# The output-gate projection taken out of the recurrence and made in ten half-width pieces between the units of the attention

## What is computed

```python
q_m, k_m, v_m, o_m, gates, q_d, k_d, v_d = project(h, w_in)       # one projection, 8 column groups
h_m = mlstm_bidirectional(q_m, k_m, v_m, gates, C0, n0, m0)       # recurrence in chunks of 128 tokens, both ways
h_d = blocked_diff_attention(q_r, k_all, v_all, lam)              # softmax map 0 minus lam * softmax map 1

def mix_output(h_m, o_m, h_d, lam_init, g_m, g_d, w_out):
    hm = head_rmsnorm(h_m).reshape(B, S, MLSTM_WIDTH) * g_m * jax.nn.sigmoid(o_m)
    hd = head_rmsnorm(h_d).reshape(B, S, DIFF_WIDTH) * g_d * (1.0 - lam_init)
    return jnp.concatenate([hm, hd], axis=-1) @ w_out
```

## Time and profile before

| what | us |
|---|---|
| median of three runs | 767.49 (765.44 to 768.3) |
| the profiled execution, its own time | 762.14 |
| its span | 760.3 |
| PE busy over the span | 671.4 (88%) |
| DVE busy over the span | 377.6 (50%) |
| recurrence, first group's scores to last group's values | 169.08 to 339.39 |
| attention, from there to the first product of the output projection | 339.39 to 419.21 |

### The profile page before, as it was taken

The page is one execution under the profiler, slowest core; times in us unless marked ns, Lnnn a source line. Parts: engine busy times, 40 slices in busy tenths (PEclk is TensorE's granted clock), DMA queues, the critical chain, the costliest instruction groups (busy, mean ns, idle before and its releaser), DMA issues.

```text
span 760.3 us, 7675 instructions
## 1 busy us (share of the span) xinstructions
PE 671.4 (88%) x2660; PEld 363.1 (48%) x2660; DVE 377.6 (50%) x784; ACT 169.1 (22%) x413; POOL 143.0 (19%) x153
## 2 busy tenths in 40 slices
PE   3899999999999999995789989992999999999920
PEld 3343573355555555443567544552544444444420
DVE  3226533413545522668987256668244423444238
ACT  6001100011212111114677221122022111221123
POOL 1042000022021100002632100003133113332061
PEclk9999999999999999998999999996899999999965
DMA  8999708422140302104000395001599999999357
GB/s 295 386 285 328 283 2 302 170 74 79 28 139 15 126 26 81 44 0 167 0 2 0 150 369 201 28 28 43 172 359 333 355 350 375 364 342 352 128 192 277
DMA packets 63058, 137.88 MB, mean 181 GB/s; under 512 B 4678, under 2 KB 11198, under 8 KB 63028
## 3 DMA queue, kind: packets, MB, share of 16 engines
q1 hardware_dynamic: 52344, 109.80, 40.9%
q0 software_dynamic: 5280, 15.63, 5.9%
q10 hardware_dynamic: 5404, 12.06, 4.0%
HBM read 122.70 MB, written 14.74 MB: 181 GB/s over the span
## 4 chain that ended last, share of the span: by engine, by line
PE 73%; DVE 11%; DMA 6%; issue 4%; ACT 2%; POOL 1%; SPq 1%; ACTq 0%; POOLq 0%; DVEq 0%
PE PS L1504 26%; PE PS L1821 15%; PE PS L1836 7%; PE PS L1496 5%; PE PS L1699 3%; DMA PR<-in_w_ada 3%; PE PS L1535 2%; PE PS L1688 1%; DVE PR L1003 1%; DMA PR<-scratch_mod 1%; PE PS L1618 1%; DVE stat L1136 1%; PE PS L1814 1%; PE PS L1592 1%; PE PS L1743 1%
## 5 line engine op out<-in xcount | busy, mean ns | idle before, releaser
L1504 PE MATMUL PS<-RING,hT 128*128 128x512 f32 x480 | 216.4, 598 | 0.8 <-DVE hT L959 0.8
L1504 PEld LDWEIGHTS PS<-RING,hT 128*128 128x128 f32 x480 | 88.1, 191 | 101.9 <-issue 101.3
L1821 PE MATMUL PS<-PR,RING 128*128 128x512 f32 x256 | 113.6, 596 | 0.0
L1821 PEld LDWEIGHTS PS<-PR,RING 128*128 128x128 f32 x256 | 47.6, 191 | 54.9 <-issue 53.8
L1699 PE MATMUL PS<-RING,hT 128*128 128x512 f32 x160 | 73.5, 611 | 0.0
L631 POOL TENSOR_TENSOR RING<-RING,PR 128x1024 f32<-128x1024 f32 x16 | 37.8, 2363 | 129.6 <-ACT RING L877 121.8
L1836 PE MATMUL PS<-PR,RING 128*128 128x512 f32 x128 | 57.6, 592 | 0.0
L1699 PEld LDWEIGHTS PS<-RING,hT 128*128 128x128 f32 x160 | 30.1, 196 | 33.2 <-issue 33.2
L1364 DVE SCALAR_TENSOR_TENSOR RING<-RING,HM,PS 128x256 f32<-128x256 f32 x16 | 7.7, 480 | 77.0 <-ACT RING L872 77.0
L1496 PE MATMUL PS<-hT,RING 128*128 128x512 f32 (+3 forms) x128 | 37.1, 450 | 0.0
L1836 PEld LDWEIGHTS PS<-PR,RING 128*128 128x128 f32 x128 | 23.7, 190 | 26.8 <-issue 26.8
(11 more groups left out here) (331 smaller groups left out, 937.2 us busy)
## 6 DMA issues: line engine op xcount, KB each, us to landing
PR<-in_w_gate_up SPq DMA_DIRECT2D x16, 2048.0 KB, 10.1
PR<-in_w_ada SPq DMA_DIRECT2D x20, 1024.0 KB, 10.3
PR<-in_w_down SPq DMA_DIRECT2D x16, 1024.0 KB, 10.7
RING<-in_w_in SPq DMA_DIRECT2D x14, 1024.0 KB, 7.4
scratch_y<-RING ACTq DMA_DIRECT2D x16, 512.0 KB, 7.5
RING<-in_w_out SPq DMA_DIRECT2D x4, 1024.0 KB, 6.3
TMP<-scratch_gfr SPq DMA_DIRECT2D x10, 256.0 KB, 5.0
scratch_h<-HM SPq DMA_DIRECT2D x5, 512.0 KB, 2.7
```

The costliest lines, as they stand in the source:

```text
L1504: last = mm(PS[:, bank, :], hTv[:, k, t * P:(t + 1) * P], ring[:, ci % 2, k, :], start=(k == 0), stop=(k == KD - 1))
L1821: last = mm(PS[:, 4 + b, :], xgT[:, b, k, :], gub[b][:, k, :], start=(k == 0), stop=(k == KD - 1))
```

## The change

The five mo units leave the list of units. Fifteen units (15 to 29, counted as `NW` = 30 with those before) fill the ten groups, three for two groups: an even group has unit a and the first half of unit a+1, the odd group behind it the second half of a+1 and unit a+2. The mo projection is made in ten **pieces** (`PIECES`): one token tile and 256 of the 512 columns each, eight products, in half a bank (bank 7's upper half; piece 1 in bank 6's lower half). Pieces 0 and 1 stand behind the scores of attention unit 1, piece 2+i behind the scores of unit 3+2i (`PIECE_AT`), so the last stands in unit 17. In those units ACT does both exponentials first and then `piece_out` (exp(-x) of the piece), and only then the copy of the transposes; PE's value product waits for `piece_out`. DVE does the 1/(1+x) of a piece (`sigmoid`) two units later, at units 3, 4, 5, 7, 9, ..., 19, ahead of its copy of the fifth transpose. POOL's two multiplications by norm and gate (`mnorm`) stand apart behind the squares of units 3, 5, 9, 13 and 17, the last in front of the squares of units 18 and 19. On SP the loads of the residual gates (`load_rows`) move ahead of the last weight chunk, which now waits for the last piece; the loads of `mbuf` for groups 7 and 8 move one chunk.

```diff
-    MB_AFTER = {3: (0, 1), 4: (2, 3), 5: (4, 5, 6), 6: (7, 8, 9)}
+    MB_AFTER = {3: (0, 1), 4: (2, 3), 5: (4, 5, 6, 7), 6: (8, 9)}
+    NW = NT * (len(WIN_ORDER) - 1)
+    PIECES = [(t_, 256 * hf_) for t_ in range(NT) for hf_ in range(2)]
+    PIECE_AT = {3 + 2 * i_: 2 + i_ for i_ in range(len(PIECES) - 2)}
+    SIGMOID_AT = {3: 0, 4: 1, **{u_ + 2: p_ for u_, p_ in PIECE_AT.items()}}
+    NORM_AFTER = {3: 0, 5: 1, 9: 2, 13: 3, 17: 4}
...
+            if ci == WOUT + 1:
+                load_rows()
+                sp.wait_ge(mm_done, NW + len(PIECES))
...
+        def mnorm(t):
+            pool.wait_ge(head_rstd, 1)
+            pool.wait_ge(sg_ready, t + 1)
...
                 osquare(h * NT + j)
+                if h * NT + j in NORM_AFTER:
+                    mnorm(NORM_AFTER[h * NT + j])
...
+        def piece_out(p_):
+            t, lo = PIECES[p_]
+            act.wait_ge(mm_done, NW + p_ + 1)
+            nc.scalar.activation(sgo[:, t, lo:lo + 256], PS[:, 6, 0:256] if p_ == 1 else PS[:, 7, 256:512], ACT.Exp,
+                                 scale=-1.0).then_inc(mm_evac, 1)
...
+            if u < NU and late:
...
+                exp_map(u, 0)
+                exp_map(u, 1)
+                piece_out(PIECE_AT[u])
...
+        def sigmoid(p_):
+            t, lo = PIECES[p_]
+            v_ = sgo[:, t, lo:lo + 256]
+            dve.wait_ge(mm_evac, NW + p_ + 1)
+            step(V.tensor_scalar(v_, v_, 1.0, None, ALU.add))
+            step(V.reciprocal(v_, v_))
...
+            if u in SIGMOID_AT:
+                sigmoid(SIGMOID_AT[u])
...
+            if odd:
+                proj(unit_a + 1, 1)
+            else:
+                proj(unit_a, 0)
...
+        def piece(p_):
+            t, lo = PIECES[p_]
+            dst = PS[:, 6, 0:256] if p_ == 1 else PS[:, 7, 256:512]
+            for k in range(KD):
...
+                last = mm(dst, hTv[:, k, t * P:(t + 1) * P], ring[:, (WOUT - 1) % 2, k, lo:lo + 256],
+                          start=(k == 0), stop=(k == KD - 1))
...
+            if u in PIECE_AT:
+                if u >= 4:
+                    pe.wait_ge(od_ready, u - 3)
+                piece(PIECE_AT[u])
...
+                if u in PIECE_AT:
+                    pe.wait_ge(mm_evac, NW + PIECE_AT[u] + 1)
```

More of the change, by code:

```diff
@@ L424, in load_ada2, with load_rows @@
                              w_late[hf, :, :, n_ * 512:(n_ + 1) * 512]).then_inc(late_in[n_ % 2], 16)
+        rows = scratch["mod"]
+        def load_rows():
+            sp.wait_ge(hm_ready, 1)
+            sp.wait_ge(row_stored, 16 * 8)
+            for c in range(2):
+                sp.dma_start(g1b[:, c, :], rows[c, 0:D].partition_broadcast(P)).then_inc(g1_loaded, 16)
+                sp.dma_start(vrows[16 * c:16 * c + 16, :], rows[c, D:3 * D].rearrange("(j p) -> j p", p=P)).then_inc(vec_loaded, 16)
         def load_mb(g):
@@ L788, in _ @@
                                      ACT.Copy).then_inc(aT4_ready, 1)
-            if u < NU:
+            if u < NU and not late:
                 act.wait_ge(smax, u + 1)
@@ L801, in _ @@
                                      ).then_inc(od_ready, 1)
-            if u < NU:
+            if u < NU and not late:
                 exp_map(u, 1)
+            if u < 2:
+                piece_out(u)
             if u == NT:
@@ L1602, in _ @@
                 last.then_inc(upd_done, 1)
-            if g >= 1:
+            if g >= 2 and not odd:
                 heads_T(unit_a - 1)
-            proj(unit_a, 1)
+            if odd:
+                proj(unit_a + 2, 0)
+            else:
+                proj(unit_a, 1)
             if g < NUPD:
@@ L1667, in _ @@
                 pe.wait_ge(a_ready, v + 1)
+                if v == 0:
+                    pe.wait_ge(mm_evac, NW + 2)
                 if v >= 1:
```

71 lines of the change are left out of this document (34 added, 37 removed).

## The result

The changed kernel takes 760.19 us (median of nine runs, 755.99 to 762.62), the kernel before 764.17 us (nine runs, 762.28 to 768.3). The ratio is 0.9938, with a 95% interval of 0.9917 to 0.9959: 4.7 us less (the two medians lie 4.0 apart), where the forecast had 7.0 less. The forecast time of 760.5 is met more closely than the forecast gain, because the kernel before came out at 764.17 us over nine runs and not at the 767.49 of the first three; that is luck.

The account below looks back on a forecast made before the run. PE was taken to bound the recurrence, PE and DVE both nearly fill the attention. Recurrence -31.9 and attention +24.9 gave -7.0: 762.14 becomes 755.1, or 760.5 from the median 767.49; range 753.5 to 769.5 us.

Parts of the forecast that it names:

- Recurrence, -31.9: Recurrence: nine gate halves of 3.43 us leave, idle PE goes, together -32.9; one new wait adds 1.0 us.
- the one new wait: Recurrence after group 1: ACT issues three output DMAs before copying out a unit to be rotated; 1.0 us, ends 0 and 3.43.
- The moved loads: Recurrence and attention: group 4's mask hidden by about 2.5 us, last output-weight chunk by 5 us or so; no cost.
- keeps its own length: Rival: something other than PE sets the recurrence, groups 0.9 us longer, time stays at 767.5; 0.22 together with late loads.
- Attention, 104.7: From the recurrence's last values to the output projection: work, pieces and waits sum to 104.7 us against 79.8, +24.9.
- PE's other work: Attention: PE's work without the change, 60.03 us busy less 1.6 for passes at half clock, 58.4 us.
- ten pieces: Attention: ten pieces of 16 passes at 0.217 us, 3.47 us each, 34.7 us in all.
- waits at the start: Attention: PE waits about 2.0 us in unit 3 and 1.6 in unit 5, together 3.6; ends 0 and 6.03.
- steady units: Attention units that run evenly: DVE has the time, so 1.5 us of PE waits in all.
- tail: End of the attention: 2.0 us for DVE's copy behind unit 19's sigmoid, 3.2 for POOL's last multiplications; 5.2, ends 0 and 7.
- hand-overs: Attention: hand-overs between engines that the walk through the units counts as nothing, 1.3 us.
- sigmoids in series: Rival: DVE's sigmoid delays maxima, exponentials and value product in units with a piece; eight pay 1.98 us, 772.7 us; chance 0.15.

Follow-up runs that it names:

- ten_products: Changed kernel with two of each piece's eight products made a second time (gate wrong): attention 115.1 us, for 106.7.
- one_more_recip: Changed kernel with a second reciprocal in the sigmoids of pieces 2 to 8 on DVE (gate wrong): attention 115.8 us, for 106.7.
- before_late: Kernel before with the last gate unit's sigmoid moved in two halves behind the differences of attention units 0 and 1: ratio 1.0005.
- before_no_recip: Kernel before without the reciprocal of its last gate unit's sigmoid (gate partly wrong): attention 77.3 us, for 79.8.
- one_product: Changed kernel with only one of the eight products left in each piece (gate wrong): attention 110.7 us, for 106.7.
- tail_copy: Changed kernel with DVE's copy of the fifth transpose ahead of the last sigmoid at unit 19: 757.31 us, ratio 0.9894.
- tail_pool: Changed kernel with PE's four transposes of the last normed tile moved behind the loop: 755.11 us, ratio 0.9876.
- tail_last: Changed kernel with last sigmoid at unit 21, POOL's last pair behind square 19, its transposes between output projection products: 753.56 us, ratio 0.9829.
- no_recip: Changed kernel without the reciprocal of the ten sigmoids on DVE (gate wrong): touched stretches 242.0 us, for 244.8.
- the three kernels at 0.98: Changed kernel with unit 19's copy ahead of the last sigmoid, with the last tile's transposes behind the loop, and with both: 757.31, 755.11, 758.24 us.

## Why the prediction came out as it did, step by step

**Recurrence, -31.9.** Right in size and nearly in detail: 170.3 to 138.1 us is -32.2. Groups take 14.32 and 14.75 us, but group 2 takes 15.96, over the 15.5 that the prediction named as a sign of being wrong; 1.00 of it is the wait that it had put there itself. PE is idle for 1.0 us, and the one new wait, 1.00 us, is where it was put, behind ACT's third output DMA (1.57 us, ending at 198.52; ACT's next copy starts at 198.62). No values waited in any group: DVE's scaling ended 0.32 us or more ahead of them. The moved loads cost PE nothing. The rival "keeps its own length" is out.

**Attention, 104.7.** It took 106.7. By the terms of the sum:

| term | forecast | measured |
|---|---|---|
| PE's other work | 58.4 | 59.9 (95.4 less the pieces) |
| ten pieces | 34.7 | 35.5 (7.10 for the first two, 3.55 for each other) |
| waits at the start | 3.6 | 2.4 (1.21 + 0.35 + 0.80) |
| steady units | 1.5 | 2.6 (six waits of 0.20 to 0.58) |
| tail | 5.2 | 5.5 (0.26 + 2.06 + 2.73 + 0.44) |
| hand-overs | 1.3 | 0.9 (the rest of 11.3 idle) |

The waits together were forecast at 11.6 and are 11.3, with 1.2 too much at the start against 1.1 too little in the steady units: luck in part. **The terms that came out too small are those of PE's work**, by 2.3 us: the pieces by 0.8, and the other work by 1.5. A pass was priced rightly (0.216 us measured), but the second pass of each piece starts 0.32 us behind the first, so a piece takes 3.56 and not 3.47 us. The 1.5 us lie in the units with a piece: unit by unit, PE is busy there for some 0.2 us longer than in the kernel before plus the 3.56 of the piece, 1.4 us in eight units, while units without a piece agree to 0.1 us. The 1.6 us taken off for matmuls at half clock was fair: PE was busy for 3.8 us at 0.50 there, of which half, 1.9 us, is lost against the full clock.

**Why a unit with a piece costs more than the piece.** The prediction set the chain of maxima and exponentials, 3.53 us, against piece and transposes, 3.94, and let the value product find the exponential done by 0.4 us. (The 0.88 in that chain is 0.79 in the earlier trace rows.) From unit 7 on that chain is indeed done in time. But the exponential reads the piece and starts only behind it, a wait that the prediction left out. So every value product of the eight units stops for it: 0.13 us in units 9 to 15, 0.46 in units 7 and 17, where one transpose stands ahead of it and not four, and 1.21 and 0.80 in units 3 and 5, where the chain itself is late. It then starts anew (eight passes in 1.13 us, for 1.06 in the kernel before). In u=11 the piece so costs 3.87 us.

**-7.0 in all, -4.7 measured** (-5.3 in the touched stretches of the two traces). The forecast of a gain was right, its mechanism too: PE's work is moved and not saved, and the gain is idle time. The output projection was to start near 412 and started at 416.0; 2.1 us of that is the longer stretch ahead of the recurrence.

**What the argument got right for a wrong reason.** It said that PE has 9.9 us in two units against DVE's 7.4, hence room. ten_products bears out the first half. one_more_recip goes against the second: 1.75 us more on DVE should have fitted in every pair, and in three of seven it did not, about 6 us in all. Busy time in a pair of units isn't room; the sigmoid stands ahead of a copy that PE's next transposes need, and the three waits are for that copy. The rival "sigmoids in series" did not happen here, with no wait over 0.46 us in front of a value product of units 7 to 17, but little more work on DVE brings on some of its waits.

**The tail** was forecast as two separate waits of 2.0 and 3.2 us. Both are there (2.06, 2.73), but they aren't separate: each alone can be removed, and both removals together take away 1.1 us of idle time and gain nothing, since DVE's chain comes out late elsewhere.

**What the old stall was worth.** The 6.03 us of the earlier trace rows was counted as gone, which it is. But moving that sigmoid alone gains 0.6 us (before_late): in that head DVE is the bound, as before_no_recip bears out (3.35 us less on DVE, 4.8 less idle time on PE). It is the pieces' time on PE that gives DVE room there, which the prediction didn't say: in units 0 to 4 PE is idle for 1.4 us with whole pieces and for 5.8 us in one_product (304.76 to 325.68).

## What to carry to other kernels

When PE work moves from one full stage into another, count it in full on both sides and look for the gain in idle time alone: here 18.1 us of it became 12.3, and then 7.6 with the last units in a better order. A wait at the end of a pipeline is removed by taking work out of the chain behind it, here by putting the last sigmoid, multiplications and transposes under the next stage's products; reordering inside the chain gained 0 to 1.3 us in the touched stretches. When an engine's result goes through another engine and back, as the piece's does, count that round trip as a wait of every unit, however short. Judge such changes stage by stage, with busy, idle and clock apart.

## What the runs showed of the hardware

**Behind some waits PE's clock falls to its lower level, and behind others not.** In the attention the granted clock is 1.00 (2.4 GHz) apart from spells at 0.50 (1.2 GHz), and every table row with a mean below 1.00 has such spells. In tail_copy the clock fell behind the wait of 2.73 us (the row of 1.91 us at 413.84), in tail_pool behind the 2.06 us that it shares with the changed kernel, whose clock stayed at 1.00 behind waits of 2.06 and 2.73. tail_last and no_recip lost waits and stayed at 1.00. So it is not shown that taking a wait away lowers the clock; each kernel has one trace, and what decides it stays open here. What it costs shows as busy time: 1.1 to 1.6 us in the three kernels at 0.98, 16.4 us in one_product at 0.83.

**The same code ahead of the recurrence took from 166.7 to 173.4 us.** Its first stretch in one_product, and in tail_copy:

```profile
0.00:166.70 166.70, 150.78 (x658) 74.46 (x659) 64.22 (x120) 25.87 (x50) 25.84 (x46) 1.00 0.68 237
```

```profile
0.00:173.40 173.40, 158.19 (x657) 77.62 (x658) 64.22 (x120) 25.88 (x50) 25.85 (x46) 0.95 0.66 229
```

DVE, ACT and POOL are busy for the same time to 0.01 us; PE's clock is 1.00 in one and 0.95 in the other. That is more than the change itself is worth. The runs of one kernel spread over 9 us (before, 759.99 to 769.31); how much of that comes from this stretch no run shows. The recurrence takes 138.1 us with the new order and 170.3 with the old in every trace, to 0.1 us.
